# A two-block network on one core: the state-space block with its steps in another order

## The reference

```python
u = (h @ w_in).reshape(bsz, seq, N_GROUPS, SSM_GROUP)      # 64 groups of 16
dt = exp(log_dt); mag = exp(a_re * dt)
ab_re = mag * cos(a_im * dt); ab_im = mag * sin(a_im * dt)
...                                                         # bb = f * b, complex
bu_re = einsum('blgh,gph->blgp', u, bb_re)                  # 64 states per group
bu_im = einsum('blgh,gph->blgp', u, bb_im)
_, _, s_re, s_im = associative_scan(combine, (ab_re, ab_im, bu_re, bu_im), axis=1)
y = einsum('blgp,ghp->blgh', s_re, c_re) - einsum('blgp,ghp->blgh', s_im, c_im) + d_skip * u
z = gelu(y) @ w_glu
return z[..., :D_MODEL] * sigmoid(z[..., D_MODEL:])
```

## Time and profile before

| | |
|---|---|
| time, median of 3 runs | 2449.91 us (2448.09 to 2449.93) |
| the profiled execution, its time | 2450.76 us |
| the profiled execution, its span from first to last instruction | 2449.0 us |
| busy PE / PEld / DVE / ACT | 2269.4 / 2042.7 / 1418.4 / 1022.4 us |
| mean granted TensorE clock | 0.959 of full |

### The profile page before, as it was taken

How to read it: one execution, slowest core, us unless ns; L and a number is a source line. 1 busy time by engine, 2 the same in 40 slices (tenths; PEclk the granted TensorE clock), 3 DMA queues, 4 the chain that set the end, 5 groups by cost and what they waited for, 6 DMA issues and landing times.

```text
span 2449.0 us, 36873 instructions
## 1 busy us (share of the span) xinstructions
PE 2269.4 (93%) x16336; PEld 2042.7 (83%) x16336; DVE 1418.4 (58%) x1494; ACT 1022.4 (42%) x1072; POOL 252.6 (10%) x122
## 2 busy tenths in 40 slices
PE   5879999889999999998979999999999997999998
PEld 5768997768997997996769799889879875987996
DVE  8565655476655544757653565455467586346554
ACT  3364543544443443453613344334335435233442
POOL 1000000000000000400153030030031003513000
PEclk9589999989999999999989999999999998999999
DMA  7024554514655654553310356556546433013653
GB/s 174 22 91 155 175 196 148 170 35 126 193 176 161 205 181 146 189 187 106 104 35 1 138 164 198 177 164 193 181 144 206 158 104 103 1 42 131 209 187 120
DMA packets 259270, 342.62 MB, mean 140 GB/s; under 512 B 23111, under 2 KB 169197, under 8 KB 259111
## 3 DMA queue, kind: packets, MB, share of 16 engines
q1 hardware_dynamic: 253968, 329.95, 42.0%
q0 software_dynamic: 2544, 9.08, 1.2%
q10 hardware_dynamic: 2599, 1.23, 0.4%
HBM read 338.14 MB, written 2.10 MB: 139 GB/s over the span
## 4 chain that ended last, share of the span: by engine, by line
PE 73%; DVE 13%; ACT 5%; DMA 4%; issue 3%; POOL 1%; SPq 1%; DVEq 0%; ACTq 0%; POOLq 0%
PE acc L1668 20%; PE acc L1669 19%; PE acc L1670 19%; DVE w_lo L1075 4%; PE acc L2056 3%; PE acc L2064 3%; ACT w_hi L655 2%; DMA raw<-in_w_in 2%; DMA raw<-in_ffn_w 1%; DVE qkT L1549 1%; PE trp L1668 1%; PE trp L1670 1%; PE trp L1669 1%; PE acc L2040 1%; PE acc L1813 1%
## 5 line engine op out<-in xcount | busy, mean ns | idle before, releaser
L1075 DVE TENSOR_TENSOR w_lo<-raw,w_hi 128x2048 fp32r<-128x2048 f32 (+1 forms) x316 | 738.3, 2341 | 545.5 <-ACT w_hi L655 544.9
L655 ACT ACTIVATE w_hi<-raw 128x2048 fp32r<-128x2048 f32 (+1 forms) x316 | 593.4, 1879 | 702.5 <-PE acc L1670 320.0
L1668 PE MATMUL acc<-xT_hi,w_hi 128*128 128x256 f32 x2848 | 812.9, 285 | 23.3 <-DVE w_lo L1075 12.3
L1669 PE MATMUL acc<-xT_lo,w_hi 128*128 128x256 f32 x2848 | 809.8, 284 | 0.0
L1670 PE MATMUL acc<-xT_hi,w_lo 128*128 128x256 f32 x2848 | 809.5, 284 | 0.0
L1668 PEld LDWEIGHTS acc<-xT_hi,w_hi 128*128 128x128 f32 x2848 | 550.9, 193 | 30.0 <-issue 15.6
L1669 PEld LDWEIGHTS acc<-xT_lo,w_hi 128*128 128x128 f32 x2848 | 551.1, 193 | 0.7 <-issue 0.7
L1670 PEld LDWEIGHTS acc<-xT_hi,w_lo 128*128 128x128 f32 x2848 | 550.8, 193 | 0.0
L1669 PE MATMUL acc<-w_lo,hT_hi 128*128 128x512 f32 x528 | 208.6, 395 | 0.0
L1670 PE MATMUL acc<-w_hi,hT_lo 128*128 128x512 f32 x528 | 208.6, 395 | 0.0
L1668 PE MATMUL acc<-w_hi,hT_hi 128*128 128x512 f32 x528 | 208.6, 395 | 0.0
(11 more groups left out here) (353 smaller groups left out, 2751.5 us busy)
## 6 DMA issues: line engine op xcount, KB each, us to landing
raw<-in_ffn_w SPq DMA_DIRECT2D x184, 512.0 KB
raw<-in_w_in SPq DMA_DIRECT2D x60, 1024.0 KB
raw<-in_ffn_w_up SPq DMA_DIRECT2D x88, 512.0 KB
raw<-in_ffn_w SPq DMA_DIRECT2D x40, 1024.0 KB
raw<-in_ffn_w_down SPq DMA_DIRECT2D x20, 1024.0 KB
raw<-in_ssm_w_glu SPq DMA_DIRECT2D x16, 512.0 KB
raw<-in_kv_w SPq DMA_DIRECT2D x8, 1024.0 KB
raw<-in_w_branch_a SPq DMA_DIRECT2D x8, 1024.0 KB
```

The source lines that it names most:

```text
L655: A(w_hi[:, p % SPL, 0:kt, :], raw[:, p % RAW, 0:kt, :], ACT.Copy).then_inc(hi_ready, 1)
L1075: V_.tensor_tensor(w_lo[:, p % SPL, 0:kt, :], raw[:, p % RAW, 0:kt, :], w_hi[:, p % SPL, 0:kt, :].bitcast(F32), ALU.subtract).then_inc(lo_ ...
L1668: mm(out, ah, bh, start=first, stop=False, skip_group_check=True)
L1669: mm(out, ah, bl, start=False, stop=False, skip_group_check=True)
```

## The change

It does seven things, all in the mixer. Both halves of the first GEMM stand next to each other on PE, ahead of the transposes of c. SP issues the second panel ahead of the parameters, b ahead of panel 2, c and all other parameters after panel 3. `Bm` is turned lag by lag for the first four tiles (`BT` has four uses instead of one for each f), each lag behind three `stay_warm` products and before that lag's responses of all eight tiles, which all go into `trp[0]` and are copied once, to `lags`. Each later `turned_inputs` starts with one `stay_warm` product. `uT` is read in phases: the 64 chunks stand in `bu`, `V1`, `V2` and `E` in the order (q c), with q the chunk number modulo 8, so that every level of the tree reads and writes runs of eight values; for that, most `advance` calls have their two multiplications in two halves (real, imaginary). DVE makes each set of `CA` just ahead of a group's `advance`, instead of all four ahead of the first. `Kbd` is filled for two tiles at once, 32 copies instead of 64. `b_n` and `bdw` move into the memory of `bu`.

```diff
-            def mixer_parameters():
+            def input_map():
+                for r, name in enumerate(("ssm_b_re", "ssm_b_im")):
+                    sp.dma_start(b_n[:, r, :, :], ...
+            def output_map():
                 for r, name in enumerate(("ssm_c_re", "ssm_c_im")):
...
-                if p == 1:
-                    mixer_parameters()
-                if p == RAW:
+                if p == 2:
+                    input_map()
+                if p == 4:
+                    output_map()
                     parameters()
...
@@ scalar
-            gemm("ssm_in0", ssm_in(0))
+            ssm_in(0)(0, use["ssm_in0"])
+            split_hi(3)
+            ssm_in(1)(0, use["ssm_in1"])
...
-            gemm("ssm_in1", ssm_in(1))
+            split_hi(4)
+            act.wait_ge(sem("bdw_in"), 16)
+            A(bdw_hi[:, :, :, :], bdw[:, :, :, :], ACT.Copy).then_inc(sem("bdw_hi_ready"), 1)
+            for lag in range(4):
+                u = use["BT"] + lag
+                wait_filled(act, u)
+                A(BT[:, :, lag], ..., ACT.Copy).then_inc(*freed(u))
+                if lag == 1:
+                    split_hi(5)
+            act.wait_ge(sem("bdw_ready"), 1)
+            act.wait_ge(sem("K_ready"), 4)
+            A(lags.rearrange("p f l h -> p (f l h)"), trp[0][:, :], ACT.Copy).then_inc(sem("lags_ready"), 1)
...
             for f in range(8):
                 driven(f)
                 if f + RING < 8:
                     turned_inputs(f + RING)
+                if f == 1:
+                    split_hi(6)
...
+            for h in range(4):
+                if h:
+                    act.wait_ge(sem("within_done"), 2 * h)
                 for g in range(8):
-                    A(Kbd[:, f % 2, :, g * GH:g * GH + GH], v, ACT.Copy, scale=const(C_PAIR + g, 1)).then_inc(sem("Kbd_ready"), 1)
+                    A(Kbd[:, :, :, g * GH:g * GH + GH], lags[:, 2 * h:2 * h + 2], ACT.Copy, scale=const(C_PAIR + g, 1)).then_inc(sem("Kbd_ready"), 1)
@@ vector
-            for p in range(4, SPL + 4):
-                split_lo(p)
+            split_lo(5)
+            split_lo(6)
             dve.wait_ge(sem("CT_ready"), 1)
-            for j in range(Q):
+            def output_rows(j):
                 step(tt(wide[0], CT[:, :, :, :], bc(bc(W[:, A1 + j, 0, :], 1, 2), 3, GH), ALU.mult))
...
             for g in range(4):
+                output_rows(g)
                 dve.wait_ge(sem("bu_copied"), 4 * (g + 1))
...
-            dve.wait_ge(sem("K_ready"), 32)
+            dve.wait_ge(sem("K_ready"), 4)
+            wait_filled(dve, use["BT7"])
@@ tensor
             features("ssm_in0", 0, use["ssm_in0"], xT, ready=xT_ready("mix0"))
+            features("ssm_in1", 0, use["ssm_in1"], xT)
...
-                            ins = mm(parts_of_bu(f, k)[:, r * NC_:(r + 1) * NC_], BT[rows, f % RING, lag, r, :], uT[rows, f, 3 - lag::4],
+                            ins = mm(parts_of_bu(f, k)[:, r * NC_:(r + 1) * NC_], BT[rows, f % RING, lag, r, :], u_phases[rows, f, :, :, 3 - lag],
...
+            u_phases = uT[:, :, :].rearrange("p f (c q j) -> p f q c j", c=8, q=8)
+            pe.wait_ge(sem("CT_ready"), 1)
+            for lag in range(4):
+                stay_warm(claim(use["BT"] + lag), 3)
+                pe.wait_ge(sem("Bm_ready"), lag + 1)
+                a = claim(use["BT"] + lag)
+                for f in range(RING):
+                    for r in range(2):
+                        at = (2 * f + r) * P
+                        ins = nc.tensor.transpose(a[:, at:at + P], Bm[:, lag, r, 4 * f:4 * f + 4, :].rearrange("p k c -> p (k c)"), ident)
+                ins.then_inc(acc_ready, 1)
+                if lag == 3:
+                    pe.wait_ge(sem("Dsel_ready"), 1)
+                response(lag)
...
-                pe.wait_ge(sem("Kbd_ready"), 8 * (f + 1))
+                pe.wait_ge(sem("Kbd_ready"), 8 * (f // 2 + 1))
```

More of the change, by code:

```diff
@@ L321, in build @@
         gemm_uses("ssm_in0")
+        gemm_uses("ssm_in1")
         uses("CT", 2)
         uses("ftab", 1)
-        gemm_uses("ssm_in1")
-        for f in range(RING):
-            uses(f"BT{f}", 1)
+        uses("BT", 4)
         for f in range(8):
@@ L1308, in _ @@
                 do(tt(CA[:, j], wide[0], wide[1], ALU.add))
[L1309 removed]
             def advance(to, old, new, power, ks=slice(0, PAIRS)):
[L1313 to L1317 removed]
+                n, c = ks.stop - ks.start, to.shape[-2] * 8
+                t1, t2 = (tmpv[:, i, 0:2 * n * c].rearrange("p (r k q c) -> p r k q c", r=2, k=n, c=8) for i in range(2))
+                q = c // 8
+                for r in range(2 if q > 1 else 1):
+                    rs = slice(r, r + 1) if q > 1 else slice(0, 2)
+                    shape = [P, rs.stop - rs.start, n, q, 8]
+                    step(tt(t1[:, rs], old[:, rs], bc(bc(bc(W[:, power, 0, ks], 1, shape[1]), 3, q), 4, 8), ALU.mult))
+                for r in range(2 if q > 1 else 1):
+                    rs = slice(r, r + 1) if q > 1 else slice(0, 2)
+                    other = old[:, 1 - r:2 - r] if q > 1 else old[:, ::-1]
+                    step(tt(t2[:, rs], other, bc(bc(W[:, power, 1:3, ks][:, rs], 3, q), 4, 8), ALU.mult))
+                step.settle(2 if q > 1 else 1)
                 do(tt(t1, t1, new, ALU.add))
@@ L1344, in _ @@
                 ks = slice(8 * g, 8 * g + 8)
[L1345 removed]
+                advance(E[:, :, ks, 1::2], E[:, :, ks, 0::2], bq[:, :, ks, 0::2], A4_, ks)
                 dve.sem_inc(sem("E_ready"), 1)
@@ L1826, in _ @@
                     turned_inputs(f + RING)
-            def response(f):
-                if f >= TRP:
-                    pe.wait_ge(sem("Kbd_ready"), 8 * (f - TRP + 1))
-                o = trp[f % TRP][:, 0:Q * GH].rearrange("p (l h) -> p l h", l=Q)
-                for lag in range(Q):
-                    for r in range(2):
-                        for k in range(4):
-                            rows, pair = slice(32 * k, 32 * k + 32), 4 * f + k
-                            mm(o[rows, lag, :], Bm[:, lag, r, pair, :], CT[:, r, pair, :], start=lag == 0 and r == 0, stop=r == 1, skip_group_check=True)
-                for k in range(4):
-                    rows = slice(32 * k, 32 * k + 32)
-                    mm(o[rows, 0, :], ident[:, rows], Dsel[:, f, :], start=False, stop=True, skip_group_check=True).then_inc(sem("K_ready"), 1)
-            pe.wait_ge(sem("CT_ready"), 1)
-            pe.wait_ge(sem("Dsel_ready"), 1)
-            pe.wait_ge(sem("bu_copied"), 16)
-            for f in range(TRP):
-                response(f)
             for f in range(8):
@@ L1867, in _ @@
                             rows = slice(32 * k, 32 * k + 32)
-                            ins = mm(y[rows, :, j], CAm[:, f % RING, j, r, k, :], E[:, r, 4 * f + k, :], start=False, stop=r == 1, skip_group_check=True)
+                            ins = mm(y[rows, :, :, j], CAm[:, f % RING, j, r, k, :], E[:, r, 4 * f + k], start=False, stop=r == 1, skip_group_check=True)
                             if j == Q - 1 and r == 1:
```

102 lines of the change are left out of this document (50 added, 52 removed).

## The result

The changed kernel takes 2464.25 us (median of 5, 2461.11 to 2467.76), the kernel before 2449.91 (median of 5 on the same chip, 2445.07 to 2453.94): ratio 1.0062, 95% interval 1.0045 to 1.0079. It is slower by 14 us, where 13 us faster was forecast. The profiled execution of the changed kernel took 2464.25 us, with a span of 2462.5.

A forecast was written before the change was run, and what follows sets the result against it. It saw a serial relay PE to ACT to DVE, mostly at 1.2 GHz, as the bound. Gains of 5.4 + 4.85 + 3.4 less 0.3 and 0.3, 13.1 us, took 2449.91 to 2436.8 us, range 2431 to 2448.

The forecast's parts named there:

- The GEMM halves together: First GEMM on PE: both halves run without a pause, first over near 35.1 us, second near 46.7, `CT_ready` near 50.6.
- The loop over the lags: PE's warm-ups, transposes and responses for four lags, with skip terms and hand-overs: 21.2 us, so `driven(0)` starts at 71.8.
- Driven at the full clock: PE's `driven` loop at 2.4 GHz: 1.75 us each, 9.0 us a pair instead of 12.9, ending at 96.8 instead of 113.9.
- Rival 1: PE's clock stays at 1.2 GHz in `driven`, which ends at 118.3 us; whole 2447.1 us; chance 0.20.
- Panel 6: DVE idles some 20 us, splits panel 6 by 86.1 us, then needs 26.0 to end `V1` at 112.1: 5.4 us gained.
- After the first level: Scan tree after `V1`: 4.85 us wait for responses goes, runs of eight save 3.4, halved multiplications and later groups cost 0.6.
- `Kbd`, the clear and the first four `CAm` hidden: ACT's work behind `driven`, from 97.6 us, ends near 125, ten us ahead of `E_ready`, so it costs nothing.
- Everything after shifts as a whole: From the first product with `w_glu` on, the rest of the kernel keeps its length and only starts earlier.
- Rival 3: Splitting panel 6 comes another 6 us later through a late load behind ACT's table store: 2442 us; within the first case's 0.72.
- Rival 2: PE reads the `driven` operand in steps of 32, which costs enough to make the kernel slower, 2467 us; chance 0.05.

The follow-up runs named there:

- experiment 9: The changed kernel with the second GEMM half put back behind the table product and c loaded with b: 2462.34 us, ratio 1.0053 to the kernel before.
- experiment 1: The changed kernel with the 1 MB table store issued behind the loop of driven products: 2455.88 us, ratio 1.0017 to the kernel before.
- 6: The kernel before with only its 1 MB table store moved behind the driven loop: 2459.98 us, ratio 1.0032 to the kernel before.
- 11: The changed kernel with the table stored twice, the second time into memory that nothing reads: 2479.71 us in one execution.
- 2: The changed kernel without its 12 + 4 warm-up products in the lag loop and the input-map transposes: 2451.47 us, ratio 1.0021 to the kernel before.
- 7: The changed kernel with the store behind the driven loop, no warm-ups in `turned_inputs`, and `CAm` cleared inside ACT's waits: 2448.29 us, ratio 0.9987 to the kernel before.
- 8: The kernel of 7 also without the twelve warm-up products of the lag loop: 2442.23 us, ratio 0.9958 to the kernel before.
- experiment 5: The kernel before with only the phase layout of the scan and the split `advance` passes: 2445.15 us, ratio 0.9982 to the kernel before.
- 3: The changed kernel with ACT's rounding of panel 6 moved behind the copy of the fourth lag: 2461.75 us, ratio 1.0054 to the kernel before.
- Experiment 4: The changed kernel with the loads of panels 7 and 8 held until the across products of eight feature blocks: 2460.34 us, ratio 1.0050 to the kernel before.

## Why the prediction was wrong

- **The GEMM halves together** (first half near 35.1, both near 46.7, `CT_ready` near 50.6): right, the lag loop starts at 50.56. It was worth less than the 11.7 us by which the loop starts sooner than the transposes of `Bm` did (62.27): against the old order with the new loads it is 3.9 us (experiment 9). And it uncovered the store.
- **The loop over the lags, 21.2 us: the step that failed.** It took 32.2. I added up the MATMULs at 0.010 us each and asked only what data they wait for. 6.47 + 2.56 us are waits for instructions, a resource that the sum had at nothing, and 1.6 the slow warm-ups behind the first gap. That the store causes the first is shown by experiments 1 and 9, which remove it, 6, which moves it, and 11, which lengthens it; that it works through the instruction packets is read from their times. The store's cover, the second GEMM half, was moved away by the very edit that I counted as a gain, and I did not name what it covered.
- **Driven at the full clock, 9.0 us a pair**: the clock held for the last six `driven` (1.00 from 98.1 to 115.5, 2.03 to 2.10 us each, 1.84 from one to the next, not 1.75), but the first pair took 15.2 us at 0.55. Here lie the next 6.2 us. Which clock `driven` gets differs from kernel to kernel without a rule that I could read: 1.00 in the last six here, 0.50 in the last four of experiment 1, 0.50 in nearly all of 2, 7 and 8. Rival 1 had the mechanism of the first pair, at 0.20.
- The Trainium skill's rule in "TensorE: Matmul & The Clock Gate", Part 4, that transposes do not count as busy for the clock: the rows neither contradict nor isolate it. The half clock of the first pair stands behind a gap and transposes, but the last six `driven` hold the full clock with transposes between them (1.04 us for eight), so by that rule alone the time would not have come out.
- **Panel 6** (86.1, DVE idle some 20 us): 103.3 and 36.7 idle. The shape was right; it inherited 11.0 + 6.2 us. From there DVE took 25.6 us to the end of `V1` (26.0 forecast).
- **After the first level**: no wait for the responses, 0.69 and 1.29/2 us on the way down, 24.2 us from `V1` to `E_ready` where it was 31.9: 7.7 gained, 7.95 forecast. Of this the way down alone is 3.1 us in experiment 5, with the layout and nothing else of the change.
- **`Kbd`, the clear and the first four `CAm` hidden, done near 125**: done at 150.1. They started 18.5 us later (116.1, not 97.6), and a TensorE tile pair took 4.9 us, not 3.0, at a mean clock of 0.51 to 0.61. Hidden by 3 us; in experiments 1, 2 and 3 TensorE waits for `CAm` instead, and ACT is the bound.
- **"Everything after shifts as a whole"**: wrong by 6.7 us. From the first product with `CAm` to the split it is 27.2 us instead of 20.5: gaps of 0.47, 1.67 and 3.77 (before 0.97 and 1.40), and a slow clock behind the third. Experiment 4 takes 3.1 of it away by moving two loads. What is left there is a gap of the kind that stands in the lag loop with nearly idle DMA engines; why some executions have it and others not is open.

Together 11.0 + 6.2 - 0.3 + 6.7 = 23.6 us, from 13.1 ahead to 10.5 behind. The whole kernel lost 14.3, 3.8 more than that mark. That is inside the spread of the executions, and not explained here. Rival 3 (panel 6 later, the stall moves) came nearest in kind, naming even the table store, but through the load of the panel, which was late and cost nothing, and not through instructions; it gave 2442. Rival 2's 2467 lies nearest to 2464 in number, by luck: its mechanism, a dear operand in steps of 32, did not occur (experiment 5).

## What to carry to other kernels

When an edit moves a dense stretch, ask what it covered: here a 1 MB store that costs at most 1.2 us beside 96 large products (`driven(0)` in experiment 6) costs 9 us beside 500 tiny ones. Count instructions per microsecond as a resource of their own, and when a gap is named "issue", look in the DMA view for what keeps the instruction queue waiting. A mark that has not moved can hide a gain and a loss of the same size, as in experiment 6, and one that has moved can owe it to the clock, as in experiment 5: look at the waits between. Warm-up products are path time; take them out once to see whether they pay.

## What was not expected of the hardware

- TensorE's instructions arrive in DMA packets of 16 KB, each 0.9 to 1.3 us long in the part shown of the changed kernel's trace, some 127 MATMULs with their weight loads in each. While a 1 MB store in rows of 512 bytes held the DMA engines at a share of 0.7, none came for 15.3 us (48.8 to 64.1), and TensorE stood still for 6.47 to 11.69 us; in another place, 12.8 us without one and 8.25 us still.
- Even with nearly idle DMA engines, responses of 0.010 us each outrun the supply: gaps of 1.2 to 2.6 us, at the same product in several kernels (2.56, 2.33, 2.28 us at the end of the lag loop). From the start of a packet to TensorE going on it is some 2.4 us (79.1 to 81.45), and its 127 responses last 1.3.
- A MATMUL of `driven` at the full clock is 0.029 us apart from the next (64 in 1.84 us from start to start), at half 0.053 (3.41): not quite half.
- A gap costs more than its length: 6.47 us of it, and 1.6 more on the six warm-up MATMULs behind it, at the half clock.
